# One more seven-product unit in each MLP of a two-block transformer, and all gate modulation tiles in the first quarter

## What is computed

```python
def sqrelu_mlp(h, w1, w2):
    return jnp.square(jax.nn.relu(h @ w1)) @ w2
...
        sh1, sc1, g1, sh2, sc2, g2 = jnp.split((silu_c @ w_mod[i] + b_mod[i])[:, None, :], N_MOD, axis=-1)
...
        x = x + g1 * rms_norm(y_lat, norm_g[i, 1])
        x = x + g2 * rms_norm(sqrelu_mlp(modulate(rms_norm(x, norm_g[i, 2]), sh2, sc2), w_mlp_in[i], w_mlp_out[i]), norm_g[i, 3])
...
        h2 = rmsnorm(x, g_mlp[l])
        u = jax.nn.relu(jnp.einsum('bsd,df->bsf', h2, w_up[l]))
        x = x + jnp.einsum('bsf,fd->bsd', u * u, w_down[l])
```

## Time and profile before

| what | value |
|---|---|
| time, median of 3 runs | 2055.35 us (2054.82 to 2057.37) |
| the profiled execution | 2052.5 us |
| its span on the core | 2050.7 us |
| granted clock of PE, mean | 0.992 |
| PE matmuls | 8777, of which 7944 in linear layers |
| first MLP | 241 to 957 us |
| second MLP | 1362 us to the end |

### The profile page before, as it was taken

The page is one execution under the profiler, slowest core; times in us unless marked ns, Lnnn a source line. Parts: engine busy times, 40 slices in busy tenths (PEclk is TensorE's granted clock), DMA queues, the critical chain, the costliest instruction groups (busy, mean ns, idle before and its releaser), DMA issues.

```text
span 2050.7 us, 23289 instructions
## 1 busy us (share of the span) xinstructions
PE 1994.3 (97%) x8777; PEld 1618.6 (79%) x8777; DVE 1543.5 (75%) x1640; ACT 1083.0 (53%) x1381; POOL 238.8 (12%) x473
## 2 busy tenths in 40 slices
PE   3999999999999999999999999999999999999998
PEld 1777568888788888887788888888888888888887
DVE  7989876767887887867556656656697887978875
ACT  3333535544555655555666755555455655655554
POOL 0000012001103112030100100000003113031130
PEclk9999999999999999999999999999999999999999
DMA  9999998879756657575556555466656667566573
GB/s 400 405 401 376 348 376 296 302 262 316 235 190 208 232 196 232 199 267 165 179 179 199 172 193 174 157 188 211 217 195 215 223 202 231 186 207 233 195 253 116
DMA packets 201498, 488.61 MB, mean 238 GB/s; under 512 B 17680, under 2 KB 24272, under 8 KB 192304
## 3 DMA queue, kind: packets, MB, share of 16 engines
q1 hardware_dynamic: 184784, 461.15, 65.1%
q0 software_dynamic: 15440, 22.57, 3.7%
q10 hardware_dynamic: 1168, 3.46, 0.4%
HBM read 461.94 MB, written 4.19 MB: 227 GB/s over the span
## 4 chain that ended last, share of the span: by engine, by line
PE 85%; DVE 6%; DMA 6%; ACT 2%; issue 1%; ACTq 0%; DVEq 0%
PE ps L614 21%; PE ps L615 20%; PE ps L616 20%; PE ps L644 7%; PE ps L645 7%; PE ps L646 7%; DVE scr L1653 3%; DMA raw<-in_fnet_w 2%; DMA raw<-in_w_mod 2%; DVE w_low L1640 2%; DMA raw<-in_w_mlp_in 1%; DVE scr L1668 1%; ACT w_high L1141 1%; PE ps L796 0%; PE ps L755 0%
## 5 line engine op out<-in xcount | busy, mean ns | idle before, releaser
L1270 ACT ACTIVATE w_high<-raw 128x1024 fp32r<-128x1024 f32 x392 | 414.4, 1060 | 400.7 <-PE ps L616 204.8
L1843 DVE TENSOR_TENSOR w_low<-raw,w_high 128x1024 fp32r<-128x1024 f32 x392 | 477.8, 1221 | 163.3 <-ACT w_high L1270 157.1
L1640 DVE TENSOR_TENSOR w_low<-raw,w_high 128x1024 fp32r<-128x1024 f32 x320 | 386.8, 1221 | 236.3 <-ACT w_high L1141 235.7
L1141 ACT ACTIVATE w_high<-raw 128x1024 fp32r<-128x1024 f32 x320 | 333.3, 1056 | 377.4 <-PE ps L616 260.5
L614 PE MATMUL ps<-w_high,u_high 128*128 128x512 f32 x1152 | 449.9, 391 | 0.7 <-DVE u_low L2250 0.7
L616 PE MATMUL ps<-w_high,u_low 128*128 128x512 f32 x1152 | 448.8, 390 | 0.0
L615 PE MATMUL ps<-w_low,u_high 128*128 128x512 f32 x1152 | 448.8, 390 | 0.0
L614 PE MATMUL ps<-w_high,h_both 128*128 128x512 f32 x896 | 357.8, 399 | 8.0 <-DVE w_low L1640 6.4
L616 PE MATMUL ps<-w_high,h_both 128*128 128x512 f32 x896 | 351.5, 392 | 0.0
L615 PE MATMUL ps<-w_low,h_both 128*128 128x512 f32 x896 | 351.4, 392 | 0.0
L560 POOL DMA_DIRECT2D extra<-scr x384 | 187.7, 497 | 1099.8 <-DVE scr L1957 977.2
(11 more groups left out here) (236 smaller groups left out, 1784.3 us busy)
## 6 DMA issues: line engine op xcount, KB each, us to landing
raw<-in_w_mod SPq DMA_DIRECT2D x96, 1024.0 KB, 7.3
raw<-in_w_mlp_in SPq DMA_DIRECT2D x64, 1024.0 KB, 5.7
raw<-in_w_mlp_out SPq DMA_DIRECT2D x64, 1024.0 KB, 5.2
raw<-in_w_up SPq DMA_DIRECT2D x64, 1024.0 KB, 5.3
raw<-in_w_down SPq DMA_DIRECT2D x64, 1024.0 KB, 5.2
raw<-in_w_in SPq DMA_DIRECT2D x48, 1024.0 KB, 5.1
raw<-in_fnet_w SPq DMA_DIRECT2D x16, 1024.0 KB, 7.0
raw<-in_w_out SPq DMA_DIRECT2D x16, 1024.0 KB, 5.1
```

The lines of the kernel that those rows point to most:

```text
L1141: eng.activation(w_high[:, h % LEAD, :], raw[:, slot, (h % 2) * 2 * CW:(h % 2 + 1) * 2 * CW], ACT.Copy).then_inc(high_ready, 1)
L1270: eng.activation(ring(w_high, h % LEAD, 1 if part == 3 else 2), raw_blocks(slot, kind, part), ACT.Copy)\
L1640: eng.tensor_tensor(w_low[:, h % LEAD, :], raw[:, slot, piece], w_high[:, h % LEAD, :].bitcast(f32), ALU.subtract).then_inc(raw_used if h ...
L1843: eng.tensor_tensor(ring(w_low, h % LEAD, count), raw_blocks(slot, kind, part), ring(w_high, h % LEAD, count).bitcast(f32), ALU.subtract). ...
```

## The change

- In each MLP one more unit is made by seven products: unit 3 in the first and unit 1 in the second. Only one unit there stays plain behind it (`first_unit`, 16 slots): unit 2, unit 0. The order becomes up(plain), up(fast), down, up(fast), down and so on.
- The token sums for the seven products are made in slots 4 to 10 of that plain unit (`COMBOS_AT = 8`).
- All 16 modulation tiles of g2 are read in the first quarter, behind two of every three chunks, from chunk 9 on. The rows are summed ahead of the plain unit.
- POOL issues all 16 DMAs of every exchange behind the first quarter; SP has none there any more. The second column of the plain unit is taken behind slot 5 of the fast unit (`LATE_TAKE = 5`).
- `kept` is issued behind the third column's exchange in place of the first's.

```diff
-MOD_FIRST = (8, 11, 14, 17, 20, 23, 26, 29)
-MOD_AFTER = (0, 1, 3, 4, 6, 8, 9, 11)
+MOD_FIRST = (7, 8, 10, 11, 13, 14, 16, 17, 19, 20, 22, 23, 25, 26, 28, 29)
+
...
-FIRST_SLOTS = 4 * HALVES + DOWN_SLOTS
-FIRST_COMBOS_AT, COMBOS_AT = 36, 24
-ROWS_AT = 27
+COMBOS_AT = 8
+PLAIN_UP = 2 * HALVES
+LATE_TAKE = 5
...
-            for pos in range(6 * NC - 2):
-                ch = pos + 2
-                if ch < 4 * NC:
-                    mlp_chunk(w_mlp_in, w_mlp_out, 1, ch)
-                else:
-                    c, j = divmod(ch - 4 * NC, 2)
-                    chunk(w_mlp_out, D + j * 4 * P, c * CW)
-                if pos in MOD_AFTER:
-                    mod_tile(G2, len(MOD_FIRST) + MOD_AFTER.index(pos))
-                exchange_behind(ch, SYNC_GROUPS)
-            for e in range(4, 2 * QUARTERS):
+            for ch in range(2, 2 * NC):
+                mlp_chunk(w_mlp_in, w_mlp_out, 1, ch)
+            for e in range(3, 2 * QUARTERS):
                 for m in range(HALVES):
                     up_chunk(w_mlp_in, e, m)
                 down_chunks(w_mlp_out, e - 1)
-            t.add("blocks", 2 * NC)
...
-            for ch in range(4 * NC):
+            for ch in range(2 * NC):
                 mlp_chunk(w_up, w_down, 0, ch)
-                exchange_behind(ch)
-            for ch in range(2 * NC):
-                c, j = divmod(ch, 2)
-                chunk(w_down, j * 4 * P, c * CW)
-                exchange_behind(4 * NC + ch)
+            for m in range(HALVES):
+                up_chunk(w_up, 1, m)
+            down_chunks(w_down, 0)
...
-            for n in range(2 * NC):
+            for n in range(NC):
                 exchange(n, n + 1, POOL_GROUPS)
-                if n == 0:
+                if n == 2:
                     eng.dma_start(kept, xs[:, :, :]).then_inc(xs_kept, 16)
-            for n in range(2 * NC, QUARTERS * NC):
+            for n in range(NC, QUARTERS * NC):
                 exchange(n, n + 1, range(QUADS))
-            eng.wait_ge(combined, 4 * 8)
+            eng.wait_ge(combined, 5 * 8)
             eng.wait_ge(xs_kept, 16)
...
+            for n in range(QUARTERS * NC, 2 * QUARTERS * NC):
+                if n == 2 * QUARTERS * NC - 2:
+                    eng.wait_ge(combined, (5 + 7) * 8)
                     eng.dma_start(grow[:, :], g_final.broadcast_to([P, D])).then_inc(grow_in, 16)
-                exchange(n, (QUARTERS + 1) * NC + n + 1, range(QUADS))
...
-            def fast_up(pairs):
+            def fast_up(pairs, plain=False):
 
                 def before(n):
-                    if n in (0, 2):
+                    if plain and n in (0, 2):
+                        eng.wait_ge(up_taken, t.c["up"] - (n == 0))
+                    elif n in (0, 2):
...
-            def up_columns(mods=(), turn_end=False):
-                for y, (c, hh) in enumerate(QUARTER_ORDER[:4 * HALVES]):
+            def up_columns(count, turn_end=False):
+                for y, (c, hh) in enumerate(QUARTER_ORDER[:count * HALVES]):
...
-                    if y % 2 and y // 2 - 2 in mods:
-                        t.add("raw")
-                    if mods and y == ROWS_AT:
-                        eng.wait_ge(raw_used, t.used())
-                        sum_partitions_to_rows(G2)
-                t.add("up", NC)
+                t.add("up", count)
...
-            up_columns(MOD_AFTER)
+            eng.wait_ge(raw_used, t.used())
+            sum_partitions_to_rows(G2)
+            up_columns(2)
             eng.wait_ge(mod_cols, G2 + 1)
-            fast_down(2, plain=True)
             eng.wait_ge(combos_low, 1)
-            for e in range(4, 2 * QUARTERS):
-                fast_up(first_combos)
+            for e in range(3, 2 * QUARTERS):
+                fast_up(first_combos, plain=e == 3)
                 fast_down(e - 1)
...
-            fast_down(0, plain=True)
+            up_columns(2, turn_end=True)
             eng.wait_ge(combos_low, 2)
-            for e in range(2, 2 * QUARTERS):
-                fast_up(combos)
+            for e in range(1, 2 * QUARTERS):
+                fast_up(combos, plain=e == 1)
                 fast_down(e - 1)
...
-            def fast_body(behind, scaled):
-
-                slots = FAST_SLOTS + behind
-                for i in range(SLOTS_ALL):
+            def fast_body(behind, scaled, steps=(0, 1)):
+
+                slots = len(steps) * (FAST_UP + FAST_DOWN) + behind
+                for i in range(len(steps) * STEP):
                     fast_high(*slots[i + LEAD])
-                    step, j = divmod(i, STEP)
+                    n, j = divmod(i, STEP)
+                    step = steps[n]
+                    if len(steps) == 1 and i == LATE_TAKE:
+                        take_exchanged(1, t.at("pool_moved", 0), pool=True)
                     if j == COPY_AT:
...
-                t.add("done", SLOTS_ALL)
+                t.add("done", len(steps) * STEP)
                 t.add("pool_moved", 4 * SHARE)
-                t.add("summed", 2 * NC)
-
...
-            def first_eighths(pairs, at, scaled, mods=()):
-
-                for y in range(FIRST_SLOTS):
-                    if y + LEAD >= FIRST_SLOTS:
-                        fast_high(*FAST_SLOTS[y + LEAD - FIRST_SLOTS])
+                t.add("summed", len(steps) * NC)
+
+            def first_unit(pairs, at, scaled):
+
+                for y in range(PLAIN_UP):
+                    if y + LEAD >= PLAIN_UP:
+                        fast_high(*FAST_UP[y + LEAD - PLAIN_UP])
                     else:
                         high_part()
-                    if y % 2 and y // 2 in mods:
-                        t.add("raw")
                     if y == at:
                         if not scaled:
                             eng.wait_ge(xs_kept, 16)
                         split_combos(pairs)
                     if y in TAKES:
-                        take_exchanged(TAKES[y], t.c["moved"], shared=not scaled)
+                        take_exchanged(TAKES[y], t.c["pool_moved"], pool=True)
...
+                t.add("done", PLAIN_UP)
...
-            first_eighths(first_combos, FIRST_COMBOS_AT, False, MOD_AFTER)
+            t.add("pool_moved", SHARE * NC // 2)
+            first_unit(first_combos, COMBOS_AT, False)
+            fast_body(FAST_SLOTS, False, (1,))
             fast_body(FAST_SLOTS, False)
...
-            first_eighths(combos, COMBOS_AT, True)
+            first_unit(combos, COMBOS_AT, True)
+            fast_body(FAST_SLOTS, True, (1,))
...
-            def fast_body(target, behind):
-
-                slots = FAST_SLOTS + behind
-                for i in range(SLOTS_ALL):
-                    step, j = divmod(i, STEP)
...
-                t.add("done", SLOTS_ALL)
+                    if len(steps) == 1 and i == LATE_TAKE:
+                        take_low(1)
+                t.add("done", len(steps) * STEP)
...
-            def first_eighths(target, pairs, at, mods=()):
-
-                for y in range(FIRST_SLOTS):
-                    if y - 4 * HALVES in DOWN_ADDS:
-                        add_down(target, DOWN_ADDS[y - 4 * HALVES], y + 1)
-                    if y + LEAD >= FIRST_SLOTS:
-                        fast_low(*FAST_SLOTS[y + LEAD - FIRST_SLOTS])
+            def first_unit(pairs, at, rows=False):
+
+                for y in range(PLAIN_UP):
+                    if y + LEAD >= PLAIN_UP:
+                        fast_low(*FAST_UP[y + LEAD - PLAIN_UP])
                     else:
                         low_part()
-                    if y % 2 and y // 2 in mods:
-                        mod_tile(G2, len(MOD_FIRST) + mods.index(y // 2))
-                    if mods and y == ROWS_AT + 1:
+                    if rows and y == 1:
                         mod_rows(G2, 2).then_inc(mod_cols, 1)
                     if y == at - 4:
                         sum_tokens()
...
-                t.add("done", FIRST_SLOTS)
+                t.add("done", PLAIN_UP)
...
-            first_eighths(acc, first_combos, FIRST_COMBOS_AT, MOD_AFTER)
+            first_unit(first_combos, COMBOS_AT, rows=True)
+            fast_body(acc, FAST_SLOTS, (1,))
...
-            first_eighths(xs, combos, COMBOS_AT)
+            first_unit(combos, COMBOS_AT)
+            fast_body(xs, FAST_SLOTS, (1,))
```

39 lines of the change are left out of this document (15 added, 24 removed).

## The result

| what | before | after |
|---|---|---|
| median of 5 runs each, side by side | 2055.73 us | 2065.33 us (2063.9 to 2068.33) |
| ratio, 95% interval | | 1.0051 [1.004, 1.0061] |
| profiled execution, its span | 2052.5, 2050.7 us | 2066.48, 2064.7 us |
| PE matmuls | 8777 | 8753 |

The change makes the kernel slower by half a per cent, 9.6 us by the medians.

The account below looks back on a forecast made before the run. PE, busy for 97% of the span, was taken to bound the kernel. Removal -5.4, late takes +7.6, `kept` +3.5 and clock +3.4 gave +9.1 on 2055.35, so 2064.4 us; range 2053.5 to 2072.0.

Parts of the forecast that it names:

- The removal: Two units become fast, one in each MLP: 24 matmuls fewer on PE, 5.44 us less.
- The late take: First fast unit of each MLP: PE waits at slot 10 for POOL's exchange, 3.8 us each, 7.6 us in all.
- E: The moment at which PE ends the plain unit's second column; the late take's steps count from it.
- its sign: Late take right: one PE pause of 3 to 6 us in each MLP's first fast unit.
- Plain-to-fast turn: 0: New turn from plain to fast unit: PE asks for column 1's banks after ACT's Relu is over, cost 0.
- `kept` at chunk 17: First quarter: the write of `kept` delays chunk 17 by 4.8 us against 1.26 to spare; PE stops for 3.5 us.
- a bound (2.6): Chunk 17: a modulation tile then in flight goes first, 2.6 us, making the upper bound of the stop 6.1 us.
- the ring's 5.6 us of slack: First quarter with 16 modulation tiles: raw ring leaves loads 5.6 us in place of 11; landings within 6.5 only nibble.
- rival 4: Denser first quarter stalls more than once after chunk 17: another 4 to 8 us, 2068 to 2073 us; chance 0.07.
- Rivals 1, 2 and 3: 1: both waits hidden, 2049.9 us, 0.11; 2: only late takes stall, 2057.5 to 2060.9, 0.14; 3: only `kept`, 2055.2, 0.08.
- The clock: Behind the three new PE pauses: two falls to half clock, 3.4 us (0 to 5.1).
- the low end of +3: Low end of the forecast's own range for the whole kernel: -5.4 + 5.4 + 1.3 + 1.7 = +3 us.

Follow-up runs that it names:

- square_later: later_tiles with the Square and block turn of the plain unit's second column moved behind the parts of the fast unit's slot 4; 2049.24 us, ratio 0.9969.
- later_tiles: both with the 16 modulation tiles reordered within the first quarter, sparser up to chunk 19 and denser after; 2051.07 us, ratio 0.9976.
- later_kept2: later_tiles with `kept` written behind the third column's exchange again, as in the change; 2054.49 us, ratio 0.9995.
- before_kept2: Kernel before with only `kept` moved, from behind the first column's exchange to behind the third's; 2058.83 us, ratio 1.0012.
- both: Changed kernel with the late take behind slot 10 and `kept` written at the end of the first quarter; 2056.26 us, ratio 0.9998.
- kept_end: Changed kernel with `kept` written behind the fourth column's exchange and the last modulation tile; 2063.44 us, ratio 1.0033.
- kept_small: Changed kernel with `kept` laid out in HBM in rows of 2 KB in place of 16 KB; 2070.45 us, one run.
- take10: Changed kernel with the late take behind slot 10 of the fast unit in place of slot 5; 2062.52 us, ratio 1.0032.
- before_dense: Kernel before with all 16 modulation tiles in the first quarter, at the change's positions, nothing else; 2064.03 us, one run.
- pool_first: both with all 16 DMAs of the first quarter's exchanges issued by POOL, none by SP; 2060.09 us, ratio 1.0026.
- later_take5: later_tiles with the late take back behind slot 5 in place of slot 10; 2059.63 us, ratio 1.0019.

## Why the prediction was right, and where it was not

The forecast was 2064.4 us and slower; measured were 2065.33 and slower. Slower was right, and so were both places and both waits. That the number came within a microsecond is luck: four terms were off, by up to 4.3 us, and the sum misses what the traces show by 4.7 us.

**The removal: right.** 24 matmuls and 5.4 us. `square_later`, where nothing is in the way, shows it: M1 is 5.8 us below before, 3.03 of it row sums, and M2 2.6; that leaves 2.8 and 2.6 us for 12 matmuls each, where 2.72 was worked out.

**The late take: the right mechanism, each step within half a microsecond, the sum too high.** E was 499.41 in the first MLP. POOL and ACT of after:

```profile
503.88 7.81 POOL L545 DMA_DIRECT2D extra<-scr  x16 [13.52 <-DVE scr L1940]
```

```profile
510.75 0.61 ACT L1250 ACTIVATE w_high<-extra 128x512 fp32r<-128x512 f32 x1
514.54 1.15 ACT L1193 ACTIVATE u_high<-extra 128x512 fp32r<-128x512 f32 x2 [3.18 <-DMA extra<-scr]
```

POOL began at E + 4.5 (predicted 4.2), the take at E + 15.1 (15.3), PE had slot 10 at E + 18.5 (18.7). The pause was 2.9 and not 3.8 because PE itself was late: the 0.6 us at slot 4 lie ahead of it, and what PE loses earlier it need not wait for later. In the second MLP the landing was quicker (the take at E + 14.5, with E = 1418.72) and the pause 2.0. So 4.8 us for the two, where the sum had 7.6; both pauses are under the 3 to 6 us that the prediction gave as its sign. The sentence of the Trainium skill (DMA: Bandwidth & Descriptors, Issuing engines are not separate DMA queues) that several issuers only save the issue time, usually small, is not borne out in its last words: the 7.8 us of issue are half of the 15.1.

**"Plain-to-fast turn: 0": wrong, 1.4 us.** I compared ACT's Relu with the moment at which PE asks for the banks. But not the banks were late. Relu, Square and the block turn stand ahead of the parts of slot 4 in ACT's and DVE's order, and a fast unit's first slots have only 6 matmuls. `square_later` moves them and the 0.6 and 0.8 us are gone.

**`kept` at chunk 17: the right place and cause, sized at 3.5 us where it was 7.8.** The term was made of an unchanged issue and a landing of 11.3. Both were off, and the runs separate them. Times count from the start of slot 16. PE wants slot 34 after 18 slots, 48.96 us, and ACT's and DVE's parts take 2.3 of it, so a chunk landed by 46.7 costs nothing.

| kernel | SP issues chunk 17 | lands after | is there | over 46.7 | pause |
|---|---|---|---|---|---|
| before | 38.8 | 6.5 | 45.35 | | none |
| later_tiles | 37.2 | 5.5 | 42.6 | | none |
| later_kept2 | 37.2 | 10.9 | 48.1 | 1.4 | 1.6 |
| before_kept2 | 37.2 | 10.9 | 48.1 | 1.4 | 1.6 |
| both | 41.2 | 8.0 | 49.2 | 2.5 | 2.6 |
| kept_end | 41.0 | 8.25 | 49.3 | 2.6 | 2.7 |
| kept_small | 40.8 | 12.7 | 53.5 | 6.8 | 7.0 |
| after | 41.0 | 13.3 | 54.3 | 7.6 | 7.8 |
| take10 | 41.1 | 12.8 | 53.9 | 7.2 | 6.6 |

The landings, by the view of DMA issues, of `later_tiles`, `both`, `later_kept2` and after:

```profile
raw<-in_w_mlp_out SPq DMA_DIRECT2D x1, 1024.0 KB, 5.5
```

```profile
raw<-in_w_mlp_out SPq DMA_DIRECT2D x1, 1024.0 KB, 8.0
```

```profile
raw<-in_w_mlp_out SPq DMA_DIRECT2D x1, 1024.0 KB, 10.9
```

```profile
raw<-in_w_mlp_out SPq DMA_DIRECT2D x1, 1024.0 KB, 13.3
```

Three terms: `kept` costs 5.4 us of landing (10.9 over 5.5, 13.3 over 8.0; I had 4.8, so this step held). A modulation tile still in flight, which the dense order puts there, costs 2.5. I had named it as a bound (2.6) and not taken it, though the change itself places it there. That it is the tile is borne out by all traces without `kept` beside the chunk: with a tile still on its way it landed after 7.7 to 8.3 us (`both`, `kept_end`, `before_dense`), without one after 5.5 to 6.5 (`later_tiles`, `pool_first`, before). And SP issues the chunk 2.2 us later (41.0 against 38.8), since it stands behind the third column's exchange; this I did not have. DVE turns the third column's blocks 34.6 us after slot 16 in after and 32.5 in before, and SP can't issue ahead of it; of before, then of after:

```profile
345.49 1.30 DVE L1957 STREAM_TRANSPOSE scr<-scr 128x512 f32<-128x512 f32 x2
```

```profile
346.89 1.30 DVE L1940 STREAM_TRANSPOSE scr<-scr 128x512 f32<-128x512 f32 x2
```

```profile
348.21 5.00 SPq L431 DMA_DIRECT2D extra<-scr  x8
353.26 1.58 SPq L400 DMA_DIRECT2D raw<-in_w_mlp_out  x2
```

The 2.2 us are a difference of two effects. In before_kept2, which only moves `kept`, the same turn comes at 30.8 and the issue at 37.2: `kept` leaving the first exchange gives back 1.6 us, and the dense tiles take 3.8. Against before the ledger reads 2.2 of issue and 6.8 of landing (13.3 over 6.5), 9.0 less the 1.35 us to spare (46.7 less 45.35), which is the 7.6.

The failed step is the sentence that put the dense quarter at nothing but the ring's 5.6 us of slack. It gave rival 4 a chance of 0.07. What rival 4 named, "the denser first quarter stalls more than once", is so in before_dense and pool_first, and its time, 2068 to 2073, lies above all five runs but one. In the changed kernel there is one pause, larger than I had it, and the tiles are part of it. Rivals 1, 2 and 3 are out: both waits show, and neither alone.

**The clock: right in kind, one fall short.** Three falls, not two: 1.8, 1.7 and 1.7 us (half of PE's busy time at the clock of 0.50), 5.2 for the 3.4 of the sum.

**The sum again**, from the traces: -5.4 + 4.8 (late takes) + 1.4 (turn) + 7.8 (chunk 17) + 5.2 (clock) = +13.8. The spans lie 14.0 apart; with the -0.7 ahead of slot 16 that leaves 0.9 unaccounted for, in small gaps. The forecast's +9.1 was 2.8 too high in one term and 4.3, 1.8 and 1.4 too low in three, 4.7 too low in all. Its range had a slip too: the low end of +3 was worked out with 1.3 us for `kept` and 1.7 for the clock, where the bounds given for both were 0.

The medians moved 9.6 us where the traces moved 14.0, and this gap is what made the forecast fit: before's median lay 3.2 us above its profiled run, the median of after 1.15 below its own. Single runs of one kernel spread over some 3 to 9 us. For after the part ahead of slot 16 can't be the whole reason: its profiled run has the earliest slot 16 of all the traces, 312.28, and still three of its other four runs are quicker. A stage can differ though its code is the same: the first MLP's late take paused PE for 2.9 us in after and in `kept_end`, with a fall of the clock in the first and none in the second, and M1 is 516.82 and 514.80. Whether the other runs of after lost less in their stages is open, since each kernel has one trace. What the late take costs by medians is as uneven: 8.6 us (`later_take5` over `later_tiles`), 7.2 (`kept_end` over `both`), 3.9 (after over `take10`).

**By chip medians**, from the bottom up: `later_tiles` is at -0.0024, the early take adds 0.0043, `kept` 0.0019, the dense order 0.0022 (`both` over `later_tiles`). That makes +0.0060 for the whole, where +0.0051 was measured, each with an uncertainty of 0.001: the parts nearly add up, and in this order of taking them the late take is the largest.

## What to carry to other kernels

Where one in-order queue issues both bulk loads and small urgent transfers, an added load must be charged with the wait of everything that stands behind it, not only with its own buffer: here eight more tiles in a ring with slack cost 4.4 us, by an exchange and a critical chunk issued later and a tile in flight, and 8.6 us beside a 2 MB write at its old place; the same eight in another order cost nothing. A take of a transfer must stand behind blocks ready + the issue time of all its DMAs + landing (here 4.5 + 7.8 + 2.8 us), and five slots later in program order brought back 6.6 to 8.2 us. A critical landing is best written down as a ledger (issue, landing alone, each thing in flight, the time it is wanted), since the overruns then match the pause, here within 0.2 us in all kernels but one, and within 0.6 in that (take10).

## What the hardware showed that I had not expected

- The engines' DMA queues shared by packets: with `kept` in 16 KB rows beside weights in small packets, 45 packets to 46 gave 0.74 MB to 0.08 MB. Cutting the rows to 2 KB moved the shares to 0.54 and 0.27 MB, and the landing only by 0.6 us.
- SP's own issues grew longer while `kept` was on its way: two loads at 355.93 and 358.55 us in after took 2.04 and 2.90 us of SP, where 0.34 is usual, and the eight DMAs of an exchange in before_dense 7.98 us where the same exchange takes 5.04 to 5.47 in the other kernels.
- The clock fell from 1.00 to 0.50 behind pauses of PE of 2.0, 2.1, 2.2, 2.6, 2.7, 2.9 and 3.1 us and of all longer ones, at a cost of 1.5 to 2.0 us each, in the three stages; it did not fall behind pauses of 0.6, 0.8, 1.3 and 1.6 us, nor behind one of 1.9 (the second MLP of later_take5) and one of 2.9 (the first MLP of kept_end). From 1.9 to 2.9 us it went either way. In the first part of before it fell behind 1.7 us of idle time.
